# Values by rows of tokens in two attention layers of a small transformer, on one core

## The reference

```python
def moba_mixer(h, w_qkv, w_o, cos_h, sin_h):           # block attention, 8 heads of 128
    qkv = (h @ w_qkv).reshape(bsz, s_len, 3, A_HEADS, A_HEAD_DIM)
    q = apply_rope(qkv[:, :, 0], cos_h, sin_h)
    k = apply_rope(qkv[:, :, 1], cos_h, sin_h)
    v = qkv[:, :, 2]
    # per head: causal softmax(q k^T / sqrt(128)) v; with 2 blocks the choice takes in every earlier block
    return o.reshape(bsz, s_len, A_HEADS * A_HEAD_DIM) @ w_o

def mla_mixer(...):                                     # latent attention, 8 heads
    cq = rms_norm(h @ w_dq, q_norm)                     # 512 wide
    q = (cq @ w_uq).reshape(..., B_HEADS, 128 + 64)     # 64 of them rotated
    kv = (c_kv @ w_ukv).reshape(..., B_HEADS, 128 + 128)  # c_kv is 256 wide: keys, then values
    # per head: causal softmax((q_nope k_nope^T + q_rope k_rope^T) / sqrt(192)) v
    return o @ w_o
```

## Time and profile before

| | |
|---|---|
| time, median of 3 runs | 1863.21 us (1863.05 to 1863.34) |
| profiled execution: its time, and the span of its trace | 1861.66 us, 1859.7 us |
| TensorE busy | 1842.6 us, 99% of the span |
| VectorE, ScalarE, GpSimd busy | 1318.0 (71%), 914.3 (49%), 53.6 us (3%) |
| TensorE's granted clock | 9 of 10 or more in all 40 slices |
| bytes moved | 174.64 MB, 94 GB/s |

### The profile page before, as it was taken

How to read it: one execution, slowest core, us unless ns; L and a number is a source line. 1 busy time by engine, 2 the same in 40 slices (tenths; PEclk the granted TensorE clock), 3 DMA queues, 4 the chain that set the end, 5 groups by cost and what they waited for, 6 DMA issues and landing times.

```text
span 1859.7 us, 31170 instructions
## 1 busy us (share of the span) xinstructions
PE 1842.6 (99%) x12175; PEld 1693.9 (91%) x12175; DVE 1318.0 (71%) x1742; ACT 914.3 (49%) x1386; POOL 53.6 (3%) x51
## 2 busy tenths in 40 slices
PE   8999999999999999999999999999999999999999
PEld 7899988988889899998898999989988898999888
DVE  6888862487656888882288888822888488888623
ACT  6455552355545545562255555622666464455522
POOL 0000000011100000000000000000000000000000
PEclk9999999999999999999999999999999999999999
DMA  6244343232223333333323343333221232343331
GB/s 183 80 113 113 91 115 102 79 90 72 77 57 102 91 91 106 97 104 106 108 57 108 91 113 104 102 98 104 63 63 57 69 91 84 99 112 105 109 102 47
DMA packets 339464, 174.64 MB, mean 94 GB/s; under 512 B 11070, under 2 KB 337836, under 8 KB 339372
## 3 DMA queue, kind: packets, MB, share of 16 engines
q1 hardware_dynamic: 338656, 172.25, 33.0%
q10 hardware_dynamic: 716, 1.11, 0.2%
HBM read 171.24 MB, written 2.10 MB: 93 GB/s over the span
## 4 chain that ended last, share of the span: by engine, by line
PE 85%; DVE 9%; ACT 3%; issue 2%; DMA 0%; POOL 0%; DVEq 0%; SPq 0%; ACTq 0%
PE acc L1881 19%; PE acc L1882 19%; PE acc L1883 19%; PE duo L1881 9%; PE duo L1883 9%; PE duo L1882 9%; DVE wl L1175 2%; DVE xg L1220 1%; DVE mx L1534 1%; PE acc L2147 1%; DVE probT L1555 1%; ACT prob L889 1%; DVE y L1240 1%; ACT wh L641 0%; DVE xT L1247 0%
## 5 line engine op out<-in xcount | busy, mean ns | idle before, releaser
L1881 PE MATMUL acc<-xg,wh 128*128 128x256 f32 (+1 forms) x1040 | 340.4, 327 | 2.4 <-DVE xg L1220 1.0
L1883 PE MATMUL acc<-xg,wl 128*128 128x256 f32 (+1 forms) x1040 | 336.9, 324 | 0.0
L1882 PE MATMUL acc<-xg,wh 128*128 128x256 f32 (+1 forms) x1040 | 336.8, 324 | 0.0
L1175 DVE TENSOR_TENSOR wl<-raw,wh 128x1024 fp32r<-128x1024 f32 (+2 forms) x198 | 228.9, 1168 | 126.5 <-ACT wh L641 126.2
L1882 PE MATMUL acc<-hT,wh 128*128 128x512 f32 (+1 forms) x704 | 255.2, 363 | 0.0
L1881 PE MATMUL acc<-hT,wh 128*128 128x512 f32 (+1 forms) x704 | 255.2, 363 | 0.0
L1883 PE MATMUL acc<-hT,wl 128*128 128x512 f32 (+1 forms) x704 | 255.2, 362 | 0.0
L641 ACT ACTIVATE wh<-raw 128x1024 fp32r<-128x1024 f32 (+2 forms) x198 | 194.4, 1011 | 116.4 <-PE acc L1883 71.8
L1881 PEld LDWEIGHTS acc<-xg,wh 128*128 128x128 f32 x1040 | 197.7, 190 | 20.5 <-issue 3.1
L1883 PEld LDWEIGHTS acc<-xg,wl 128*128 128x128 f32 x1040 | 197.7, 190 | 15.8
L1882 PEld LDWEIGHTS acc<-xg,wh 128*128 128x128 f32 x1040 | 197.9, 190 | 14.9
(11 more groups left out here) (283 smaller groups left out, 4175.6 us busy)
## 6 DMA issues: line engine op xcount, KB each, us to landing
raw<-in_ffn_w_dram SPq DMA_DIRECT2D x238, 512.0 KB, 4.2
raw<-in_ffn_w_dram SPq DMA_DIRECT2D x32, 384.0 KB, 3.4
raw<-in_moba_w_qkv_dram SPq DMA_DIRECT2D x24, 512.0 KB, 3.8
raw<-in_moba_w_o_dram SPq DMA_DIRECT2D x8, 512.0 KB, 3.8
raw<-in_mla_w_o_dram SPq DMA_DIRECT2D x8, 512.0 KB, 3.7
xin<-in_x_dram SPq DMA_DIRECT2D x4, 512.0 KB, 5.4
raw<-in_mla_w_dq_dram SPq DMA_DIRECT2D x4, 512.0 KB, 3.9
raw<-in_mla_w_uq_dram SPq DMA_DIRECT2D x8, 256.0 KB, 2.9
```

The source lines that it names most:

```text
L1175: v.tensor_tensor(wl[:, slot, 0:tiles], raw[:, slot, 0:tiles], f32(wh[:, slot, 0:tiles]), ALU.subtract).then_inc(w_lo, 1)
L1881: t.matmul(dst, w_h, m_h, start=start, stop=False, skip_group_check=onto)
L1882: t.matmul(dst, w_h, m_l, start=False, stop=False, skip_group_check=onto)
L1883: return t.matmul(dst, w_l, m_h, start=False, stop=stop, skip_group_check=onto)
```

## The change

All values are computed first, with the roles swapped: a block of 128 tokens is the stationary operand and 512 weight columns, four heads at once, are the moving one, so values come out with tokens on the partitions and are never transposed. In the block attention `all_values` replaces `quad`: two groups of four heads, each group four units of two weight tiles by 512 columns, 96 matmuls 512 wide. ScalarE and VectorE split them with the norm factor by token, `rtok`, as scale (`values_hi`, `values_lo`), into `oT`, which the heads' outputs overwrite later. The units then are q0, k0, q1, k1 and so on, two per head. In the latent attention four small units (four tiles) stand ahead of the heads, 48 matmuls; a head's unit has six tiles, not eight. The number of weight units of the block attention stays 24. `out_proj` gets a shorter first piece in the block attention. The core of the diff:

```diff
@@ TensorE, block attention
+            def values_product(dst, slot, k, c, start, stop):
+                (x_h, x_l), cols = from_x(xg, slice(c * P, (c + 1) * P))(k), slice(VG * (k % 2), VG * (k % 2 + 1))
+                dst = dst[:].rearrange("p (h d) -> p h d", d=P)
+                t.matmul(dst, x_h, wh[:, slot, cols], start=start, stop=False)
+                t.matmul(dst, x_h, wl[:, slot, cols], start=False, stop=False)
+                return t.matmul(dst, x_l, wh[:, slot, cols], start=False, stop=stop)
+            def all_values(xg0, n_post, n_pre):
...
+                for e in range(2):
+                    for k in range(KD):
...
+                        for c in range(HT * e, HT * (e + 1)):
+                            ins = values_product(att_banks[1][c], k // 2, k, c, k == 0, k == KD - 1)
...
+                        if (e, k) == (1, 6):
+                            mean(n_pre)
+                for e in range(2):
+                    for k in range(KD):
+                        w = u + KD // 2 + k // 2
+                        pe.wait_ge(w_lo, w + 1)
...
+                        if (e, k) == (0, 1):
+                            spread(n_pre)
-            quad(1, XG0[X_F0], N_F0, N_PRE1)
-            qkv_unit(4)
-            qkv_unit(5)
-            value_transposes(0, r + 3)
+            all_values(XG0[X_F0], N_F0, N_PRE1)
+            for h in range(2):
+                qk_unit(h, 0)
+                qk_unit(h, 1)
             for h in range(HEADS - 1):
                 moba_scores(h)
                 if h:
                     prob_transposes(h - 1, (0, 1))
-                    qkv_unit(3 * h + 4)
+                    qk_unit(h + 1, 1)
                     prob_transposes(h - 1, (2,))
-                    qkv_unit(3 * h + 5)
-                    values(h - 1)
                 if h + 2 < HEADS:
-                    if h == 0:
-                        pe.wait_ge(v_lo, 1)
-                    qkv_unit(3 * h + 6)
-                if h + 2 < HEADS:
-                    value_transposes(h + 1, r + 3 * h + 6)
+                    qk_unit(h + 2, 0)
+                    if h:
+                        values(h - 1)
@@ out_proj
                 pe.wait_ge(evacuated, att - 1)
-                pe.wait_ge(o_lo, last - 2)
-                heads_done(0, 0, HEADS - 3)
-                value_transposes(last, att)
+                if st == 1:
+                    pe.wait_ge(o_lo, last - 3)
+                    heads_done(0, 0, HEADS - 4)
+                    values(last - 2)
+                    first = HEADS - 4
+                else:
+                    pe.wait_ge(o_lo, last - 2)
+                    heads_done(0, 0, HEADS - 3)
+                    first = HEADS - 3
                 prob_transposes(last - 1, (0,))
                 last_scores()
@@ TensorE, latent attention
+            for i in range(4):
+                g, k = divmod(i, KK)
...
+                for c in range(TS):
...
+                    t.matmul(dst, ckT[:, 0, k, cols], w_h, start=k == 0, stop=False)
+                    t.matmul(dst, ckT[:, 0, k, cols], w_l, start=False, stop=False)
+                    ins = t.matmul(dst, ckT[:, 1, k, cols], w_h, start=False, stop=k == KK - 1)
...
-                head_part("k", h + 1).then_inc(head_psum, 1)
-                head_part("v", h + 1).then_inc(unit_done, 1)
+                head_part("k", h + 1).then_inc(unit_done, 1)
...
-                if h + 2 < HEADS:
-                    value_transposes(n + 1, r + mla_rr["v", h + 1] + 1)
```

More of the change, by code:

```diff
@@ L987, in rotated @@
                 part((qh, kh)[i][:, 0], (rope_q, rope_k)[i][1][:])
+            split(u + 4)
+            split(u + 5)
+            load_table(EXP)
+            for i in range(TS):
+                values_hi(i)
+            split(u + 6)
+            split(u + 7)
+            for i in range(TS, TS + HT):
+                values_hi(i)
+            for w in range(8, 11):
+                split(u + w)
             probT_zeros()
+            for i in range(TS + HT, 2 * TS):
+                values_hi(i)
+            split(u + 11)
             for i in range(2):
@@ L1083, in _ @@
             cq_hi_of(1)
+            split(u + 6)
+            cq_hi_of(2)
+            split(u + 7)
+            cq_hi_of(3)
             load_table(EXP)
-            cq_hi_of(2)
-            cq_hi_of(3)
-            split(u + 6)
+            for i in range(TS):
+                latent_hi(i)
+            split(u + 8)
+            split(u + 9)
+            for i in range(TS, 2 * TS):
+                latent_hi(i)
+            split(u + 10)
             def exchanged(gg, i):
@@ L1142, in _ @@
                     o_split(n - 1)
-                if nxt and not turn:
-                    v_split(n + 1)
             probT_split(2 * HEADS - 1, (0, 1, 2))
             o_split(2 * HEADS - 1)
-            out_proj(u + KQ + 12, N_MLA, gain(1, 3, 0))
+            out_proj(u + KQ + 16, N_MLA, gain(1, 3, 0))
             x_update(X_MLA, N_MLA, gain(1, 3, 0), U0[6], gain(1, 4, 0), N_PRE5)
@@ L1638, in _ @@
             split(u + 6)
-            evac_v(u + 3, acc[2][:])
-            rotated(0, 0)
-            rotated(0, 1)
-            products(1, 0)
-            products(1, 1)
-            split(u + 7)
-            v_split(0)
-            softmax_mask(0)
-            softmax_max(0)
-            evac_v(u + 6, att_banks[1][5][:])
-            rotated(1, 0)
-            rotated(1, 1)
-            softmax_norm(0)
-            v_split(1)
-            split(u + 8)
-            split(u + 9)
-            for h in range(1, HEADS - 1):
-                products(h + 1, 0)
+            split(u + 7)
@@ L1657, in _ @@
+            for i in range(TS, TS + HT):
+                values_lo(i)
+            for w in range(8, 11):
+                split(u + w)
+            for i in range(TS + HT, 2 * TS):
+                values_lo(i)
+            split(u + 11)
+            for i in range(2):
+                products(0, i)
+            for i in range(2):
+                rotated(0, i)
+            split(u + 12)
+            products(1, 0)
+            for h in range(HEADS):
                 softmax_mask(h)
-                probT_split(h - 1, (0, 1))
+                if h:
+                    probT_split(h - 1, (0, 1))
@@ L1673, in _ @@
-                v_split(h + 1)
-            probT_split(HEADS - 2, (0, 1, 2))
-            softmax_mask(HEADS - 1)
-            softmax_max(HEADS - 1)
-            softmax_norm(HEADS - 1)
-            o_split(HEADS - 2)
+                if h + 1 < HEADS:
+                    rotated(h + 1, 0)
+                    split(u + 13 + 2 * h)
+                softmax_norm(h)
+                if h == HEADS - 1:
+                    split(u + 27)
+                if h + 1 < HEADS:
+                    products(h + 1, 1)
@@ L1679, in _ @@
+                if h:
+                    probT_split(h - 1, (2,))
+                if h + 1 < HEADS:
+                    split(u + 14 + 2 * h)
+                    rotated(h + 1, 1)
+                if h + 2 < HEADS:
+                    products(h + 2, 0)
+                if h:
+                    o_split(h - 1)
             probT_split(HEADS - 1, (0, 1, 2))
@@ L1783, in _ @@
             products(0)
-            copy_v(0)
             for m in range(1, KQ):
```

285 lines of the change are left out of this document (160 added, 125 removed).

## The result

| | before | after |
|---|---|---|
| time, median | 1863.13 us (1861.84 to 1863.34, 4 executions) | 1889.18 us (1887.90 to 1890.63, 4 executions) |
| ratio to before, 95% interval | | 1.0141, 1.0125 to 1.0157 |
| profiled execution: time, span | 1861.66, 1859.7 us | 1890.63, 1888.7 us |
| TensorE's mean granted clock | | 0.996 |

The account below looks back on a forecast made before the run. TensorE was taken to bound the block attention until the small engines' chain takes over, and that chain to pace the latent loop. Block 11.9 plus latent 8.6 made 20.5; 1861.66 + 20.5 + 1.55 = 1883.7, say 1884, range 1871 to 1891.

Parts of the forecast that it names:

- My own case: Whole kernel: the block and latent attention both get longer, time between 1879 and 1889 us; chance 0.52.
- the rival with the clock: In the new waits TensorE's clock falls to 1.2 GHz, 2 us each time, up to 4: 1888 us; chance 0.15.
- Second value group: Block attention, fifth weight tile: unit 6 is split late, so TensorE stands idle 3.2 us.
- Scores 1: Block attention: head 1's key is rotated behind head 0's softmax; scores 1 come 14.0 us after scores 0, 6.6 idle.
- 16.05 vs 16.7: Block attention, per head: TensorE's share falls to 16.05 us, the small engines' chain takes 16.7 and binds by 0.65.
- Behind scores 7: End of the block attention: TensorE loses 2.9 us from scores 6 to 7 and waits 2.1 inside `values(6)`.
- Latent attention: Scores 0 come 9.8 us later, the loop over heads gets 1.2 us shorter; net 8.6 us longer.
- TensorE's busy time: Sign in the trace after: TensorE's busy time 8 us smaller while the span is 20 larger.
- the one that priced the clock at zero: New waits of TensorE: granted clock rows show 1.00 even after idle time, so they give no price but zero.
- TensorE's work alone: Whole kernel: only TensorE's work counts, so 7.0 us of transposes and 1.2 of `quad` are saved: 1855 us; chance 0.08.
- the shorter latent loop: Latent attention: the loop shortens with TensorE, giving 14.5 us instead of 1.2: 1871 us; chance 0.1.
- the block chain that fits: Block attention: chain links overlap by 0.7 more and unit 6 is not late, 5 to 6 us less: 1878; chance 0.12.

Follow-up runs that it names:

- fill_idle: The changed kernel with 41 more matmuls whose results nothing reads, in the two longest waits (unit 6 and scores 1); 1885.07 us (1.0120).
- unit6_early: The changed kernel with the splits of units 6 and 7 ahead of the norm factor; 1884.14 us (1.0116).
- key1_early: The changed kernel with both rotations of head 1 in front of the loop over heads, as before the change; 1883.41 us (1.0115).
- output_late: The changed kernel with the high and low part of a head's output one head later, behind the maximum; 1883.13 us (1.0113).
- both_split: The whole change with the block attention's orders mended and each head's second weight split behind the next key's parts; 1871.15 us (1.0044).
- lean_values: The kernel before, leaving out five of six value matmuls and three of four value transposes of each latent head; 1862.94 us (1.0003).
- moba_only: The kernel before with the change in the block attention alone; 1879.95 us (1.0093).
- warm_start: Only the block attention changed, its orders mended, plus 23 unread transposes of the identity at the program's start; 1859.60 us (0.9987).

## Why the prediction was right, and where it fell short

The forecast was 1884 in a range of 1871 to 1891; the time is 1889.2. My own case went from 1879 to 1889, so the time is just outside it and inside the range only because that took in the rival with the clock. Profiled execution against profiled execution the change costs 29.0 us: 1.8 in front of the block attention, 5.2 for the clock (3.7 by `fill_idle` in the block attention; 1.5 in the latent one, 15.26 less the 13.73 us of the next such interval, heads 3 to 4), and 22.0 for the waits and the work, where the sum had 20.5.

- **Second value group.** Forecast 3.2 us for unit 6, measured 3.25, by `wl`. `unit6_early` takes it away. The price of the swapped matmuls, taken over without a row, was right too (0.227).
- **Scores 1.** Forecast 14.0 behind scores 0 with 6.6 idle; measured 14.26 and 6.69, by the low part of `kh`. Right, and `key1_early` shows the order as the cause.
- **The loop over heads.** The step "16.05 vs 16.7" had the right bound. The chain measured 16.93 and TensorE's share 15.92 (`output_late`). These terms and the ones ahead put scores 7 at 10.9 us later (184.55 by `fill_idle` less the 173.66 before) instead of 9.2. The term was mis-sized, and mostly in one link: between scores 3 and 4 the steps up to the key's high part come within 0.03 us each of the forecast, but from there to its low part VectorE takes 0.97 instead of 0.81, because the weight split ahead of it ends later, and 0.74 instead of 0.69 from the low part to the scores. With TensorE's share 0.13 smaller than forecast, the chain is over it by 1.0 a head and not by 0.65.
- **Behind scores 7.** Forecast 2.9 in front of them and 2.1 inside `values(6)`; measured 2.40 and 1.69. From scores 7 to the end of the block attention it takes 2.5 us more than before, against 2.7.
- **Latent attention.** Forecast 9.8 up to the loop: the first exponential comes 53.63 us behind the statistics, against 43.96, so 9.7. The loop was to become 1.2 us shorter; from the first exponential to that of head 7 it is 0.4 longer with the clock's fall, and 1.1 shorter in `fill_idle`, without it. Together 8.6 forecast, and 8.6 where the clock held (`fill_idle`: 1883.3 less 1329.19, where its statistics stand, is 554.1, against 545.56).
- **TensorE's busy time** did not fall by 8. Matmuls at half the clock last longer, but that is not all: `both_split`, with the same 12015 matmuls and one short fall, is busy for 1837.3 us, only 5.3 less than before.
- **The step that failed** is the one that priced the clock at zero, on the ground that the first 5 us of the trace before show 1.00 with TensorE idle. The trace after shows how little that row proves: its granted clock is 1.00 too while its first matmuls start at nearly twice the distance (last section). The rival with the clock had a chance of 0.15 and 1888; it is what happened, with 5.2 us in three places, beside the waits of my own case. The other rivals fell: TensorE's work alone (it waits 11.6 us in front of scores alone), the shorter latent loop (`lean_values`), and the block chain that fits (16.93).

What stays open: why a fall follows one wait and not another. In the kernel after it followed a wait of 1.85 us and not one of 2.40; in `key1_early`, `fill_idle`, `unit6_early` and `moba_only` it followed the 2.40; the 3.25 of unit 6 had one behind it in the kernel after and none in `key1_early`. These runs show that the two filled waits had no fall behind them, not which unfilled ones will.

## What to carry to other kernels

When work is taken from the engine that is busy for 99% of the span, first work out the chain of the other engines from one loop pass to the next: here a rebuild that spared TensorE 128 of the block attention's matmuls lost 17 us there to four places in the orders of VectorE and ScalarE, and all of it came back by moving a few calls. A loop that the small engines pace returned nothing for the work taken out of it, and what was put in front of it was paid in full. A new wait of TensorE must be priced together with the slower matmuls that may follow it, here 1.3 to 2.4 us more, in some executions and not in others.

## What the runs showed of the hardware

A fall of the clock cost 1.3 us (heads 0 to 1 in `lean_values`) to 2.4 us (scores 1 to 2 after) beside the wait itself. A single wait of 1.85 us was followed by one, and so were two of 0.79 and 1.02 us close together. Matmuls whose results are thrown away were worth their place in such waits: with 41 of them scores 7 came 3.7 us earlier.

The program's start has two forms in one and the same kernel. In the trace after, the first 256-wide matmuls start 0.21 us apart for 4.4 us, although the granted clock is shown as 1.00:

```profile
11.18 0.41 PE L1918 MATMUL acc<-xg,wh 128*128 128x256 f32 x1
11.39 0.41 PE L1919 MATMUL acc<-xg,wl 128*128 128x256 f32 x1
```

```profile
10.80:15.20 4.40, 4.38 (x20) 4.40 (x21) 3.85 (x9) 4.11 (x9) 0.00 (x0) 1.00 1.15 310
```

In `warm_start` they are 0.12 apart:

```profile
10.62 0.28 PE L1932 MATMUL acc<-xg,wh 128*128 128x256 f32 x1
10.74 0.28 PE L1933 MATMUL acc<-xg,wl 128*128 128x256 f32 x1
```

Those 20 matmuls are the 1.8 us by which the trace after stands later from the start. The 1.55 us between the profiled execution before and its median most likely have the same cause: that trace has the distance of 0.12, and `lean_values`, the same kernel up to the latent attention, has 0.21 and stands 1.4 us later at the same place. So a granted clock of 1.00 in a row does not prove full speed right after idle time; the distance between the starts of matmuls does.
